# Where the plain weight tiles stand among the short ones in a fused attention block, and when the third head's attention begins

## The chip, the cores and the metric

One Trainium2 chip, one of its cores. The time is device microseconds for one execution of the whole kernel. The kernel before took 740.01 us (median of 3 runs, 738.37 to 742.52).

## The reference

`x` is 256 tokens by 2048 channels, fp32. The block computes, all in fp32 accuracy:

- `h = rmsnorm(x) * g_norm`, then one projection `z = h @ w_in` that yields q, k, v and a gate for 8 differential heads and 8 forgetting heads (head width 128), 8 forget logits and two merge gates of 2048 columns each.
- Forgetting heads: `softmax(q k^T / sqrt(128) + c_q - c_k + causal)` with `c` the running sum of the log forget gates, times v. Differential heads: rotary on 16 of 64 columns, two softmax maps, first minus lambda times second, times v, RMSNorm over the head.
- Each head's output is multiplied by SiLU of its gate; the two branches are projected by `w_proj_a` and `w_proj_b`, merged by two sigmoid gates, projected by `w_out`, added to `x`, and normalized once more.

## The kernel before

**The product.** Every fp32 product is made of three: weight and activation are each split in a high and a low part (`w_hi` + `w_lo`, `hT_hi` + `hT_lo`), and TensorE multiplies high by high, high by low, and low by high.

**The jobs.** The weights come in 326 tiles of 128 x 1024, called jobs, in one fixed order. Five parties work through this same order, each in its own instruction queue: SyncE issues the load of the raw tile (L372 to L392), ScalarE rounds it to `w_hi` (L720), VectorE subtracts to get `w_lo` (L956), TensorE multiplies by `w_hi` (L420, L421) and then by `w_lo` (L435 or L488). There are 4 places for raw tiles and 4 for split tiles. So ScalarE's split of job n + 4 waits until TensorE has finished job n, and the load into a raw place waits until VectorE has done with the job four loads earlier.

**Plain and short jobs.** In a plain job (`tile`, L423) a tile meets both halves of the tokens: 12 matmuls of 512 columns. From job 28 to job 247 the order is made of 11 chunks of 20 jobs. A chunk holds the 8 plain jobs of one head's projection, which accumulate in PSUM banks Z0 and Z1, and 12 short jobs (`sum_tile`, L454) of 6 matmuls each. The short jobs compute the merge gates and two of the heads by a scheme of seven block products (forms P1, P5, P6, P3, P7, P4, P2, four short jobs each) in place of eight. In forms P5, P6, P7 and P4 the weight tile is itself a sum or a difference of blocks, and VectorE makes it first (`add`, L963: lines L969 and L971), five jobs ahead. After some forms VectorE folds a bank into the result (L973). `HEAD_STEPS` (L49) says at which of the 20 steps the plain jobs stand; `SUM_STEPS` are the others.

**Queue order.** In the iteration of job n VectorE does, in this order: the fold if a form ended with n, the add of job n + 5 if it is one, the split of job n + 4, and its pieces of attention. ScalarE does: the evacuation of Z0 and Z1 if n is the last plain job of a chunk (L722 to L726, it waits for TensorE's end of n), the split of job n + 4, its pieces of attention.

**Evacuation.** The first plain job of the next chunk writes Z0 and Z1 again, so TensorE waits there (`banks_free`, L439) for the evacuation.

**Attention.** Each head b has a job X (`X_AT`) and a job Y (`Y_AT`), five jobs later. After job X TensorE transposes the gated output of head b - 2 (L544), the probabilities of head b - 1 (L526) and q and k of head b (L501). After Y it multiplies the values of head b - 1 (L535) and makes the scores of head b (L514, L517). At Y VectorE gates the output and takes the row maxima of the scores (L1101, L1103); one job later ScalarE takes the exponentials (L810, L812). When the maxima of a forgetting head are there, GpSimd makes the bias of the next one (L1368, L1373). For heads 3 to 15 the jobs X and Y are given by `X_ALONE`; those of heads 0 to 2 are written out.

Of the kernel before, what the change touches and what calls it, by code (L numbers as in the profile page):

```python
# [35 lines left out]
N_HEADS = 2 * HEADS  # L36
# [6 lines left out]
FOX2_JOB = FOX_JOB + 16  # L43
DIFF_JOB = FOX2_JOB + 8
# [1 line left out]
LAST_JOB = OUT_JOB + 30  # L46
JOBS = LAST_JOB + TILES

HEAD_STEPS = (0, 3, 5, 8, 10, 13, 15, 17)  # L49
SUM_STEPS = [u for u in range(MIXED) if u not in HEAD_STEPS]  # L50
FOX_STEPS, FOX_SUM_STEPS = (0, 2, 4, 5, 8, 11, 14, 15), (1, 3, 6, 7, 9, 10, 12, 13)
OUT_PLAIN = [(2, j) for j in range(TILES)] + [(0, j) for j in range(4, TILES)] + [(1, j) for j in range(4, TILES)]
# [7 lines left out]
SUM_OF = {job: s for s, job in enumerate(SUM_JOB)}  # L60
X_ALONE = {**{3 + c: MIXED_JOB + MIXED * (c + 1) + 4 for c in range(3)},
           **{b: MIXED_JOB + 3 * MIXED + 4 + 16 * (b - 5) for b in range(6, N_HEADS)}}
X_AT = {21: 0, 28: 1, 38: 2, **{job: b for b, job in X_ALONE.items()}, FOX2_JOB + 1: N_HEADS, DIFF_JOB + 1: N_HEADS + 1}
Y_AT = {25: 0, 33: 1, 43: 2, **{job + 5: b for b, job in X_ALONE.items()}, FOX2_JOB + 5: N_HEADS}

C_ZERO, C_MASK, C_TRI, C_IDENT, C_ONE = 0, P, 2 * P, 3 * P, 4 * P
C_COS, C_SIN, C_BF, C_GS, C_LAM = 5 * P, 5 * P + 16, 5 * P + 32, 5 * P + 40, 5 * P + 41
# [8 lines left out]
def head_job(h, j):  # L76
    c = ALONE.index(h)
    if c == 0:
        return j
    return PLAIN_JOB + j if c == 2 else MIXED_JOB + MIXED * (c - 3) + HEAD_STEPS[j]  # L80

# [61 lines left out]
def build(nc, x, xT, xg, consts_in, w_main, w_fl, g_final, out):  # L143
# [11 lines left out]
    with ctx:  # L155
# [262 lines left out]
        def _(pe):  # L418
# [72 lines left out]
            def head_transposes(h):  # L491

                if h < HEADS:
                    wait_z(pe, h)
                else:
                    pe.wait_ge(rope_ready, h - HEADS + 1)
                if h >= 2:
                    pe.wait_ge(og_ready, h - 1)
                for i in range(2):
                    for m in range(M_TILES):  # L500
                        mm = pe.transpose(A[:, (2 * i + m) * P:(2 * i + m + 1) * P],  # L501
                                          z_of(h)[:, m, i * HD:(i + 1) * HD], ident)
                mm.then_inc(qkT_done, 1)
# [52 lines left out]
            def attention(job):  # L556

                if job in X_AT:
                    b = X_AT[job]
                    if b >= 2:  # L560
# [3 lines left out]
                    if b < N_HEADS:  # L564
                        head_transposes(b)
                if job in Y_AT:
                    b = Y_AT[job]
                    if b >= 1:
# [140 lines left out]
        def _(act):  # L709
# [80 lines left out]
            def head_qkT(h):  # L790

                act.wait_ge(qkT_done, h + 1)
                act.activation(qk0T[:], A[:].rearrange("p (i n) -> p i n", i=2)[:, :, 0:P], ACT.Copy)
                act.activation(qkT_hi[:], A[:, P:4 * P], ACT.Copy).then_inc(qkT_hi_ready, 1)
# [5 lines left out]
            def tanh(h):  # L800

                wait_z(act, h)
                act.activation(gate_tanh[:], z_of(h)[:, :, 3 * HD:4 * HD], ACT.Tanh, scale=0.5).then_inc(tanh_ready, 1)

            def exps(h):

                act.wait_ge(max_ready, max_count(h + 1))
                maps, scale = 1 if h < HEADS else 2, -1.0
                for i in range(maps):
                    act.activation(probs[:, i, 0:P], probs[:, i, 0:P], ACT.Exp, bias=neg_max[:, 2 * i:2 * i + 1],  # L810
                                   scale=scale, accum_out=sums[:, 2 * i:2 * i + 1])
                    ins = act.activation(probs[:, i, P:3 * P], probs[:, i, P:3 * P], ACT.Exp,  # L812
                                         bias=neg_max[:, 2 * i + 1:2 * i + 2], scale=scale,
                                         accum_out=sums[:, 2 * i + 1:2 * i + 2])
                ins.then_inc(exp_done, 1)

            def out_square(h):

                act.wait_ge(o_done, h + 1)
                for m in range(M_TILES):  # L820
                    ins = act.activation(og[:, m, :], A[:, m * P:(m + 1) * P], ACT.Square, scale=inv[:, m:m + 1],
                                         accum_out=o_ssq[:, m:m + 1])
                ins.then_inc(o_squared, 1)
# [28 lines left out]
            def attention(job):  # L852

                if job in X_AT:
                    b = X_AT[job]
                    if b >= 2:
# [3 lines left out]
                    if b < N_HEADS:  # L860
                        head_qkT(b)
                if job - 2 in X_AT and 1 <= X_AT[job - 2] <= N_HEADS:
                    tanh(X_AT[job - 2] - 1)
                if job in Y_AT and Y_AT[job] > HEADS:
                    out_square(Y_AT[job] - 1)
                if job - 1 in Y_AT and Y_AT[job - 1] < N_HEADS:
                    exps(Y_AT[job - 1])

# [597 lines left out]
```

## Time and profile before

| quantity | value |
|---|---|
| median of 3 runs | 740.01 us |
| profiled execution, its own time | 740.3 us |
| its span, first to last instruction | 738.5 us |
| TensorE matmuls busy | 723.9 us (98%) |
| VectorE busy | 624.9 us (85%) |
| ScalarE busy | 462.8 us (63%) |
| GpSimd busy | 85.9 us (12%) |
| mean granted TensorE clock | 0.997 |

The span is the profiler's view of the execution; its own time is 1.8 us longer. TensorE's busy share counts matmuls from issue to their modelled end, so that neighbours overlap; a gap that is shorter than that overlap does not show as idle time. The distance from one matmul's start to the next shows it.

### The profile page before, as it was taken

What the parts mean: (1) busy time and instruction counts of PE and PEld (TensorE: products, weight loads), DVE (VectorE), ACT (ScalarE), POOL (GpSimd) and SP (SyncE); (2) the same over time, 40 slices, a digit from 0 to 9 for tenths busy, and PEclk for the clock granted to TensorE, in tenths of its full rate; (3) what the DMA queues carried; (4) which work ended last, traced back from release to release, by engine and by line L of the source; (5) the groups of instructions that cost most, each with busy time, mean ns of one, the idle gap of its engine ahead of it and who ended that gap; (6) DMA issues with size and microseconds to landing.
All of it is one profiled execution on the core that took longest, in us unless ns stands there. A gap on an engine that the chain in (4) does not pass through costs nothing.

```text
span 738.5 us, 9450 instructions
## 1 busy us (share of the span) xinstructions
PE 723.9 (98%) x3454; PEld 599.1 (81%) x3454; DVE 624.9 (85%) x788; ACT 462.8 (63%) x682; POOL 85.9 (12%) x105
## 2 busy tenths in 40 slices
PE   9999999999999999999999999999999999999995
PEld 6998887868888888888888887888877888888884
DVE  6785698897989988989889899899899667799883
ACT  7963666567575766665865667776657544555552
POOL 0000231020202051000102030111030000001030
PEclk9999999999999999999999999999999999999998
DMA  8679356769676795776966867775768655667862
GB/s 334 211 235 322 125 199 229 245 242 349 217 259 229 239 348 208 261 234 235 326 228 216 270 226 260 281 257 202 225 233 266 214 192 191 279 232 246 285 200 114
DMA packets 49822, 178.39 MB, mean 242 GB/s; under 512 B 5544, under 2 KB 5552, under 8 KB 49264
## 3 DMA queue, kind: packets, MB, share of 16 engines
q1 hardware_dynamic: 48656, 174.41, 67.9%
q10 hardware_dynamic: 864, 1.84, 0.7%
q0 software_dynamic: 256, 1.54, 0.6%
q8 instruction: 27, 0.44, 0.2%
q14 instruction: 19, 0.16, 0.1%
HBM read 175.67 MB, written 2.11 MB: 241 GB/s over the span
## 4 chain that ended last, share of the span: by engine, by line
PE 46%; issue 28%; DVE 14%; DMA 6%; POOL 3%; ACT 2%; POOLq 0%; SPq 0%; DVEq 0%; ACTq 0%
PE Z L420 13%; PE Z L421 12%; PE Z L435 10%; DVE w_lo L956 7%; DMA w_raw<-in_w_main 4%; PE Z L488 3%; DVE x_and_g L971 3%; PE Z L594 3%; POOL rope_t L1385 1%; DMA gates<-c_rows_dram 1%; ACT w_hi L720 1%; DVE w_raw L969 1%; DMA c_rows_dram<-c_neg 1%; DVE sum_lo L1090 1%; POOL o_rstd L1397 1%
## 5 line engine op out<-in xcount | busy, mean ns | idle before, releaser
L956 DVE TENSOR_TENSOR w_lo<-w_raw,w_hi 128x1024 fp32r<-128x1024 f32 (+1 forms) x238 | 291.3, 1232 | 64.5 <-ACT w_hi L720 63.2
L720 ACT ACTIVATE w_hi<-w_raw 128x1024 fp32r<-128x1024 f32 (+1 forms) x237 | 245.4, 1044 | 134.9 <-PE Z L435 74.9
L420 PE MATMUL Z<-w_hi,hT_hi 128*128 128x512 f32 (+2 forms) x640 | 242.5, 382 | 2.6 <-ACT z_sb L725 2.3
L421 PE MATMUL Z<-w_hi,hT_lo 128*128 128x512 f32 (+2 forms) x640 | 240.3, 379 | 0.0
L720 ACT ACTIVATE w_hi<-x_and_g 128x1024 fp32r<-128x1024 f32 x88 | 93.2, 1062 | 95.5 <-DVE x_and_g L971 66.6
L420 PEld LDWEIGHTS Z<-w_hi,hT_hi 128*128 128x128 f32 x640 | 120.3, 188 | 26.8 <-ACT z_sb L725 3.1
L421 PEld LDWEIGHTS Z<-w_hi,hT_lo 128*128 128x128 f32 x640 | 120.4, 188 | 21.7
L435 PE MATMUL Z<-w_lo,hT_hi 128*128 128x512 f32 (+2 forms) x512 | 129.7, 376 | 0.0
L956 DVE TENSOR_TENSOR w_lo<-x_and_g,w_hi 128x1024 fp32r<-128x1024 f32 x88 | 108.4, 1233 | 13.0 <-ACT w_hi L720 11.5
L420 PE MATMUL Z<-w_hi,sum_hi 128*128 128x512 f32 x292 | 115.4, 395 | 1.4 <-DVE x_and_g L1193 1.3
L421 PE MATMUL Z<-w_hi,sum_lo 128*128 128x512 f32 x292 | 113.8, 390 | 0.0
L435 PEld LDWEIGHTS Z<-w_lo,hT_hi 128*128 128x128 f32 x512 | 92.3, 188 | 18.2 <-DVE w_lo L956 0.8
L971 DVE TENSOR_TENSOR x_and_g<-w_raw,x_and_g 128x1024 f32<-128x1024 f32 x66 | 82.0, 1242 | 5.7 <-DMA w_raw<-in_w_main 5.6
L420 PEld LDWEIGHTS Z<-w_hi,sum_hi 128*128 128x128 f32 x292 | 54.8, 188 | 14.1 <-DVE x_and_g L1193 1.7
L421 PEld LDWEIGHTS Z<-w_hi,sum_lo 128*128 128x128 f32 x292 | 54.9, 188 | 10.8
L488 PE MATMUL Z<-w_lo,sum_hi 128*128 128x512 f32 x164 | 50.8, 391 | 0.3
L488 PE MATMUL Z<-w_lo,hT_hi 128*128 128x512 f32 x128 | 39.9, 393 | 0.6 <-DVE w_lo L956 0.5
L1397 POOL TENSOR_TENSOR o_rstd<-o_ms,neg_half 128x2 f32<-128x2 f32 x8 | 7.4, 929 | 270.3 <-DVE o_ms L1180 270.3
L488 PEld LDWEIGHTS Z<-w_lo,sum_hi 128*128 128x128 f32 x164 | 30.6, 188 | 7.5 <-DVE w_lo L956 1.1
L435 PE MATMUL Z<-w_lo,sum_hi 128*128 128x512 f32 x128 | 34.4, 390 | 0.8 <-DVE w_lo L956 0.8
L1368 POOL TENSOR_TENSOR bias<-gates,c_nat 128x128 f32<-128x128 f32 (+1 forms) x16 | 14.4, 918 | 169.3 <-DVE neg_max L1103 161.4
L969 DVE TENSOR_TENSOR w_raw<-x_and_g,w_raw 128x1024 f32<-128x1024 f32 x22 | 27.2, 1238 | 5.3 <-DMA w_raw<-in_w_main 5.2
(219 smaller groups left out, 698.5 us busy)
## 6 DMA issues: line engine op xcount, KB each, us to landing
w_raw<-in_w_main SPq DMA_DIRECT2D x295, 512.0 KB, 4.3
x_and_g<-in_w_main SPq DMA_DIRECT2D x22, 512.0 KB, 7.0
w_raw<-in_w_fl SPq DMA_DIRECT2D x8, 264.0 KB, 3.1
o_T<-in_x SPq DMA_DIRECT2D x1, 2048.0 KB, 8.0
x_and_g<-in_xT SPq DMA_DIRECT2D x4, 256.0 KB, 5.7
gates<-c_rows_dram POOLq DMA_DIRECT2D x1, 1024.0 KB, 8.4
z_sb<-in_g_final SPq DMA_DIRECT2D x1, 1024.0 KB, 10.0
x_and_g<-in_xT ACTq DMA_DIRECT2D x3, 256.0 KB, 7.3
```

The costliest lines, as they stand in the source:

```text
L420: pe.matmul(acc, a_hi, b_hi, start=first, stop=False)
L421: pe.matmul(acc, a_lo, b_hi, start=False, stop=False)
L435: mm = pe.matmul(Z[2 * pair + m][:, 0:n], stat_hi[:, k0 + kk, tok], lo[:, kk], start=False, stop=last and kk == ks - 1 and closed)
L488: mm = pe.matmul(acc[:], stationary(2 * q + kk)[0], lo[:, kk], start=False, stop=2 * q + kk == ks - 1 and (not into_tile or f != P3))
L594: mm = pe.matmul(Z[m][:], x_part[:, 2 * j + kk, m * P:(m + 1) * P], w_part[:, kk], start=(j == 0 and part == 0 and kk == 0), stop=(j == TI ...
L720: act.activation(w_hi[:, t % RING, 0:cols_of(t)], weights(t), ACT.Copy).then_inc(hi_ready, 1)
L956: dve.tensor_tensor(w_lo[:, t % RING, 0:n], weights(t), w_hi[:, t % RING, 0:n].bitcast(fp32), ALU.subtract).then_inc(lo_ready, 1)
L969: dve.tensor_tensor(raw, chain[:, q, :], raw, ALU.subtract).then_inc(added, 1)
L971: dve.tensor_tensor(chain[:, q, :], raw, chain[:, q, :], ALU.subtract).then_inc(added, 1)
L1090: dve.tensor_tensor(sum_lo[:, form], sums_raw[:, form], sum_hi[:, form].bitcast(fp32), ALU.subtract).then_inc(sums_lo_ready, 1)
L1368: pool.tensor_tensor(bias[:, sl].unsqueeze(1), rows.rearrange("p (h n) -> p h n", h=HEADS)[:, h:h + 1, 0:n], c_nat[:, m, h:h + 1].unsqueez ...
L1397: pool.tensor_tensor(o_rstd[:], o_ms[:], neg_half[:], ALU.pow).then_inc(o_rstd_ready, 1)
```

## The change

The plain jobs of a chunk stand at steps 0, 2, 5, 7, 10, 12, 14, 16 in place of 0, 3, 5, 8, 10, 13, 15, 17. Five plain jobs move one step forward, each past one short job. Steps 17, 18 and 19 are then short jobs; before, 18 and 19 were. X of head 2 is job 36 in place of 38, its Y is job 41 in place of 43. All other X and Y keep their job numbers, though some of these jobs are now short where they were plain, or the other way round.

```diff
-HEAD_STEPS = (0, 3, 5, 8, 10, 13, 15, 17)
+HEAD_STEPS = (0, 2, 5, 7, 10, 12, 14, 16)
...
-X_AT = {21: 0, 28: 1, 38: 2, **{job: b for b, job in X_ALONE.items()}, FOX2_JOB + 1: N_HEADS, DIFF_JOB + 1: N_HEADS + 1}
-Y_AT = {25: 0, 33: 1, 43: 2, **{job + 5: b for b, job in X_ALONE.items()}, FOX2_JOB + 5: N_HEADS}
+X_AT = {21: 0, 28: 1, 36: 2, **{job: b for b, job in X_ALONE.items()}, FOX2_JOB + 1: N_HEADS, DIFF_JOB + 1: N_HEADS + 1}
+Y_AT = {25: 0, 33: 1, 41: 2, **{job + 5: b for b, job in X_ALONE.items()}, FOX2_JOB + 5: N_HEADS}
```

## Rows read from the trace of the kernel before

**Rows 1.** The page's first part: busy time, share, instructions of each engine.

```profile
PE 723.9 (98%) x3454; PEld 599.1 (81%) x3454; DVE 624.9 (85%) x788; ACT 462.8 (63%) x682; POOL 85.9 (12%) x105
```

**Rows 2.** Stretches: length, busy time of each engine, granted clock, DMA share, GB/s.

```profile
77.10:121.52 44.42, 42.84 (x207) 35.55 (x206) 40.13 (x52) 30.08 (x49) 11.15 (x13) 1.00 0.51 179
121.52:164.31 42.79, 42.10 (x188) 33.12 (x189) 39.06 (x44) 26.49 (x35) 5.28 (x6) 1.00 0.70 233
164.31:204.79 40.48, 40.48 (x188) 33.80 (x189) 34.75 (x39) 26.85 (x35) 3.70 (x4) 1.00 0.75 273
410.13:452.97 42.84, 41.99 (x203) 34.56 (x202) 39.97 (x52) 27.41 (x45) 6.24 (x7) 1.00 0.73 246
495.55:537.60 42.05, 41.71 (x194) 33.39 (x193) 37.94 (x59) 28.36 (x49) 6.79 (x8) 1.00 0.65 217
```

**Rows 3.** Who waited for whom: total us, times, longest us.

```profile
PE Z L420 <- ACT z_sb L725: 2.3, 2, 1.5
PEld Z L488 <- DVE w_lo L956: 3.3, 6, 0.7
PEld Z L435 <- DVE w_lo L956: 2.0, 4, 1.2
```

**Rows 4.** Groups by shape: busy us, mean ns of one, idle before.

```profile
L956 DVE TENSOR_TENSOR w_lo<-w_raw,w_hi 128x1024 fp32r<-128x1024 f32 x230 | 285.7, 1251 | 60.9 <-ACT w_hi L720 59.7
L725 ACT ACTIVATE z_sb<-Z,rstd 128x512 f32<-128x512 f32 x25 | 15.8, 683 | 8.2 <-PE Z L435 7.2 <-POOL rstd L1353 0.9
```

**Rows 5.** Timeline, TensorE, the starts of jobs 46, 47 and 48: start, length.

```profile
117.17 0.39 PE L420 MATMUL Z<-w_hi,sum_hi 128*128 128x512 f32 x1
118.53 0.39 PE L420 MATMUL Z<-w_hi,sum_hi 128*128 128x512 f32 x1
121.52 0.47 PE L420 MATMUL Z<-w_hi,hT_hi 128*128 128x512 f32 x1 [1.47 <-ACT z_sb L725]
```

**Rows 6.** Timeline, ScalarE and VectorE, ahead of job 48.

```profile
119.28 0.40 ACT L810 ACTIVATE probs<-probs,neg_max 128x128 f32<-128x128 f32 x1 [1.41 <-DVE neg_max L1103]
120.18 1.24 ACT L725 ACTIVATE z_sb<-Z,rstd 128x512 f32<-128x512 f32 x2
122.40 1.23 DVE L956 TENSOR_TENSOR w_lo<-w_raw,w_hi 128x1024 fp32r<-128x1024 f32 x1 [2.01 <-ACT w_hi L720]
```

**Rows 7.** Timeline, TensorE after job 33 and before job 39.

```profile
91.76 0.39 PE L420 MATMUL Z<-w_hi,hT_hi 128*128 128x512 f32 x1
101.30 0.38 PE L544 MATMUL C<-consts,og 128*128 128x128 f32 x2
```

**Rows 8.** Timeline, ScalarE, the last exponential of head 1.

```profile
96.80 0.49 ACT L812 ACTIVATE probs<-probs,neg_max 128x256 f32<-128x256 f32 x1
97.20 0.19 ACT L812 ACTIVATION_READ_ACCUMULATOR probs<-probs,neg_max 128x1 f32 x1
```

**Rows 9.** Timeline, GpSimd's bias of the next head, and VectorE beside it.

```profile
96.28 1.22 DVE L971 TENSOR_TENSOR x_and_g<-w_raw,x_and_g 128x1024 f32<-128x1024 f32 x1
98.77 1.63 DVE L971 TENSOR_TENSOR x_and_g<-w_raw,x_and_g 128x1024 f32<-128x1024 f32 x1
101.80 1.41 DVE L956 TENSOR_TENSOR w_lo<-x_and_g,w_hi 128x1024 fp32r<-128x1024 f32 x1
96.45 2.87 POOL L1368 TENSOR_TENSOR bias<-gates,c_nat 128x128 f32<-128x128 f32 x2 [14.96 <-DVE neg_max L1103]
119.33 1.89 POOL L1368 TENSOR_TENSOR bias<-gates,c_nat 128x128 f32<-128x128 f32 x2 [17.21 <-DVE neg_max L1103]
```

**Rows 10.** Timeline, VectorE and TensorE in the chunk of jobs 48 to 67.

```profile
127.32 3.50 DVE L956 TENSOR_TENSOR w_lo<-w_raw,w_hi 128x1024 fp32r<-128x1024 f32 x3
131.89 1.23 DVE L969 TENSOR_TENSOR w_raw<-x_and_g,w_raw 128x1024 f32<-128x1024 f32 x1 [1.07 <-DMA w_raw<-in_w_main]
147.70 1.23 DVE L971 TENSOR_TENSOR x_and_g<-w_raw,x_and_g 128x1024 f32<-128x1024 f32 x1 [1.39 <-DMA w_raw<-in_w_main]
162.15 0.73 PE L488 MATMUL Z<-w_lo,hT_hi 128*128 128x512 f32 x2 [0.17 <-DVE w_lo L956]
```

**Rows 11.** The loads of L392 from 125 to 165 us, issue to landing.

```profile
DMA to landing us min/median/max: 3.1/4.2/6.7
```

**Rows 12.** Timeline, jobs 207 and 208: TensorE, and ScalarE's work ahead of the evacuation.

```profile
450.60 0.39 PE L420 MATMUL Z<-w_hi,hT_hi 128*128 128x512 f32 x1
452.97 0.47 PE L420 MATMUL Z<-w_hi,hT_hi 128*128 128x512 f32 x1 [0.85 <-ACT z_sb L725]
449.28 1.05 ACT L720 ACTIVATE w_hi<-w_raw 128x1024 fp32r<-128x1024 f32 x1
451.59 1.28 ACT L725 ACTIVATE z_sb<-Z,rstd 128x512 f32<-128x512 f32 x2
```

## The prediction, made before the changed kernel was run

> **What bounds the kernel now.** I read the busy times first: TensorE 98%, VectorE 85% [rows 1]. TensorE's matmuls are the same before and after, so the change can only move TensorE's waits. The stretches come next, cut at the starts of the chunks' first jobs. The third chunk (jobs 68 to 87) takes 40.48 us without a gap; the second has the same jobs and one head's attention too, but takes 42.79, so 2.31 us of it are waits; VectorE is busy 39.06 of the 42.79 us there [rows 2]. The table of waits names two kinds: TensorE for the evacuation of its banks, twice, and its weight loads for VectorE's `w_lo`, ten times [rows 3]. The timelines put a place to them. A short job takes 118.53 - 117.17 = 1.36 us; job 47 starts at 118.53, so job 48 could start at 119.89 and starts at 121.52: 1.63 lost to the evacuation [rows 5]. Job 207 starts at 450.60 and job 208 at 452.97 in place of 451.96: 1.01 lost in the same way [rows 12]. The pool that the change can reach is 1.63 + 2.31 + 1.01 = 4.95 us. The last chunk (jobs 228 to 247, 42.05 us, [rows 2]) has waits for `w_lo` too; I come to it below.
>
> **What moves.** A swapped plain job takes 2.72 us (12 matmuls, twice the short one), so between the two swapped steps TensorE is 1.36 us further on in time for the same job number, and the add of the short job is made one iteration later. At every other step the sums of TensorE time, adds and splits up to that job are what they were. So no job's `w_lo` is wanted earlier than before, and no more VectorE work stands ahead of it. The number of instructions, of loads and of bytes stays. What can change is (A) the evacuation at job 48, (B) VectorE's lateness in the second chunk, (C) the evacuation at job 208.
>
> **A, the first chunk.** ScalarE's exponentials of head 2 wait for VectorE's maxima until 119.28, and only behind them, at 120.18, comes the evacuation of 1.24 us (two of 0.68, [rows 4]) [rows 6]. With Y at job 41 the exponentials stand in iteration 42, and the evacuation in iteration 44, not 45. In its queue it then stands behind the split of job 47 (which waits for an add) and ahead of the split of job 48. Counting VectorE's queue on from 96.28 at 1.14 us for an add and 1.14 to 1.27 for a split (the pitch of such rows, 1.25 long alone, [rows 4]), the add of job 47 ends near 117, ScalarE's split near 118.2, the evacuation near 119.5 and the split of job 48 near 120.5. TensorE would want job 48 at 119.9. Three things take back from the 1.63:
> First, X of head 2. TensorE starts job 34 at 91.76 [rows 7]; with a short, a plain and a short job it now reaches X at 91.76 + 5.44 = 97.20, where before it came at 101.30 [rows 7]. It wants the exponentials of head 1 there, which end at 97.20 + 0.19 = 97.39 [rows 8]. That costs 0 to 0.3 us; I take 0.15, the nearest by these rows. VectorE's queue up to there has the same work as before.
> Second, GpSimd's bias for head 3 begins near 115.7 in place of 119.33, and VectorE is no longer idle beside it. In the row of 98.77, with GpSimd at work, an add takes 1.63 in place of the 1.22 of the row of 96.28 [rows 9]; from 96.28 to 101.72 four operations take about 1.0 us more than their pitch. The cost is 0 (the cover of before) to 1.0; I take 0.5 on TensorE's path, because jobs 46 to 48 have `w_lo` only about 1 us ahead.
> Third, nothing more for the three short jobs: TensorE needs 4.08 us for them, and ScalarE's evacuation and split take 1.24 + 1.05.
> A is 1.63 - 0.65 = 1.0 gained, between 0 and 1.63.
> At the second point a rule of the Trainium skill speaks against the change: "SBUF — State Buffer", section "SBUF: two separate sides", says that an operation of VectorE with two SBUF inputs and one of GpSimd that reads SBUF lock each other out for a whole instruction. By that, four GpSimd operations of about 0.95 us would hold VectorE for up to 3.8 us and A would be a loss of about 2 us (near 741 for the kernel). The rows show VectorE 1.0 us later over such a stretch and GpSimd's pair at 2.87 in place of 1.89, so here the delay is shared and small, and I keep the rows' price.
>
> **B, the second chunk.** VectorE bounds it: at 162.15 TensorE starts on `w_lo` of job 66 having waited for it [rows 10]. VectorE itself has three holes: 2.01 at 122.40 behind the evacuation [rows 6], 1.07 at 131.89 and 1.39 at 147.70, both for a load [rows 10]. The first goes in part with A: VectorE is some 0.9 ahead at job 49. The hole at 131.89 stays: before it was the load of job 55, issued when job 51 was split (127.32 + 1.22 = 128.54). Now the first add is for job 56, whose load is issued one split later, at 129.68 - 0.9 = 128.8; with the median 4.2 us to landing [rows 11] it starts at 133.0, but one split of before has already been done by then, so that after both adds and splits VectorE is only 0.15 ahead. The hole at 147.70 was job 62's load. Now job 61's load is issued near 139.5, lands near 143.7 and is wanted near 144.3: it closes, 1.39 gained. So `w_lo` of jobs 66 and 67 comes 0.15 + 1.39 = about 1.6 earlier, and since VectorE sets the time there, job 68 starts 1.6 earlier, of which A is 1.0 and B adds 0.6. A load takes 3.1 to 6.7 us [rows 11]: the slowest at job 61 gives 6.7 - 4.2 = 2.5 back (B is -1.9), and with no hole at all the whole 2.31 goes. I take the median.
>
> **C, job 208.** X of head 12 is job 204, before short and now the last plain job. Before, ScalarE did the split of job 208 (449.28), the four copies of attention, and then, at 451.59, the evacuation [rows 12]. Now the evacuation stands ahead of the split of 208: from about 449.4 to 450.65, and TensorE can start job 208 at 451.96. The split then ends at 451.7, and the copies (some 1.4 us) and the split of job 209 at about 454.6, just when TensorE comes there. That puts 0.1 to 0.2 on job 209. C is 1.01 - 0.15 = 0.85, between 0 and 1.0.
>
> **The rest.** In the last chunk the adds, folds and attention up to VectorE's iteration 241 are the same sum, so its waits stay: 0. The other chunk ends start without a wait.
>
> **Sum.** 1.0 + 0.6 + 0.85 = 2.45. The profiled execution's own time is 740.3, so 737.85; the median of the runs shown is 0.3 lower: 737.5.
>
> **The rivals.**
> *Data-bound second chunk.* VectorE waits for loads in place of ScalarE: what A gives is lost by job 68, and only C stays: 740.0 - 0.85 = 739.2. For it: two of the three holes are loads [rows 10], and the loads are issued by VectorE's own progress. Against it: the order of the adds after job 56 leaves each load longer.
> *All waits go.* Loads land early, GpSimd costs nothing: 740.0 - 4.95 = 735.1. For it: only 2.01 + 1.07 + 1.39 = 4.5 us of holes [rows 6, 10] keep VectorE late at job 66, and the change needs just half of them. Against it: VectorE's work in the two chunks is 40.13 and 39.06 us [rows 2], so margins stay thin.
> *Slower: the lead runs dry after three short jobs.* At step 16 ScalarE evacuates (1.24) ahead of the split of the next chunk's first plain job, and TensorE covers one plain job less (1.36): 2.6 us per chunk end where VectorE is late, and four ends are (jobs 48, 68, 208, 248). 4 x 2.6 = 10.4 lost, the evacuation waits of 2.64 gone: 747.8. It decides from 0.6 per end (2.45 / 4). Against it: my count at job 48 has the split ready at 120.5 where TensorE comes at 120.5, at 208 ready 0.3 before, so an end costs 0.2 at the most.
> *It doesn't do what it says:* something else holds ScalarE at the chunk's end, and both evacuation waits stay: 740.0.
>
> **How the numbers follow.** Forecast 0.38, data-bound 0.28, all waits go 0.22, slower 0.08, no effect 0.04. 0.5% is 3.7 us, about what a measurement can tell. Faster by more means below 736.3: all waits go, and the forecast's own lower tail (0.06), 0.28. Slower by more: above 743.7, 0.06. The rest is 0.66. The range takes in 735.1 and 739.2; upward it goes to the slow load on top of the forecast (737.5 + 2.5 = 740.0) with the 1.2 that the runs shown differ by beside it. It runs from 734.9 to 741.2.
>
> **What would show it.** Right: no wait for `z_sb` ahead of jobs 48 and 208; jobs 77.10 to 48 in about 43.4 us; the second chunk at about 42.2; X of head 2 near 97.3; the last chunk near 42.05 again. Wrong: a new wait for `w_hi` at a chunk's first job (the slower rival), or a longer hole before an add in the second chunk (the data-bound one), or X of head 2 more than 0.5 us late.

## The result, and the profile after

The changed kernel is slower: 741.27 us (median of 20 executions, 739.39 to 744.82) against 739.40 for the kernel before (20 executions, 736.97 to 743.02), a ratio of 1.0029 with a 95% interval of 1.0016 to 1.0041. Forecast was 0.3% faster; measured is 0.3% slower, 0.07 us above the range. The profiled execution of the changed kernel has an own time of 743.39 us (before 740.3), so it lies 2 us above its own median, and what it shows has to be held against the times. Two executions of e9 below (1477.67 and 1477.81 us) and one of e11 (1218.53) took far longer than all others, and the medians and ratios given there are without them. The page's first part, which answers to [rows 1]:

```profile
PE 725.2 (98%) x3454; PEld 600.0 (81%) x3454; DVE 625.4 (84%) x788; ACT 461.8 (62%) x682; POOL 82.2 (11%) x105
```

The same work. The stretches by chunk, the changed kernel, in the order of [rows 2] (first, second, third, ninth chunk, last):

```profile
77.09:119.52 42.43, 42.43 (x207) 35.69 (x206) 39.98 (x53) 30.75 (x49) 12.99 (x12) 1.00 0.52 186
119.52:163.40 43.88, 41.71 (x190) 33.25 (x188) 39.66 (x44) 25.90 (x35) 5.59 (x4) 1.00 0.72 240
163.40:203.88 40.48, 40.48 (x189) 33.80 (x189) 34.58 (x38) 27.39 (x36) 3.63 (x4) 1.00 0.73 260
410.20:453.43 43.23, 42.51 (x204) 34.48 (x202) 39.01 (x52) 26.17 (x41) 5.26 (x7) 1.00 0.71 243
495.99:538.31 42.32, 41.81 (x194) 33.47 (x193) 39.19 (x58) 28.35 (x49) 8.22 (x12) 1.00 0.65 229
```

Against [rows 2]: the first chunk is 1.99 shorter, the second 1.09 longer, the third equal, the ninth 0.39 longer, the last 0.27 longer. Between them one job (158) came 0.94 late, as single jobs do with either order (with the old one job 159 lost 1.29 in the profile of e2 below). That makes 0.71 in sum, by which job 248 starts later. The rest of the 3.09 us between the two profiled executions comes behind the last chunk. The waits of the changed kernel, from its table (total us, times, longest):

```profile
DVE x_and_g L971 <- DMA w_raw<-in_w_main: 9.6, 7, 2.5
DVE w_raw L969 <- DMA w_raw<-in_w_main: 5.9, 5, 2.2
PEld Z L488 <- DVE w_lo L956: 4.9, 6, 1.8
PEld Z L435 <- DVE w_lo L956: 3.7, 5, 1.2
PE Z L420 <- DVE x_and_g L1193: 2.4, 1, 2.4
```

TensorE's wait for `z_sb` [rows 3] is gone from the table: both evacuations are early enough. On the other side its weight loads wait longer for `w_lo` (8.6 us in place of 5.3), and VectorE's adds wait for loads from memory. A wait of 2.4 us stands ahead of job 256, where the kernel before has 1.3 (below).

**The first chunk** did what the change says. Timelines of the changed kernel: TensorE at X of head 2 and at job 48, ScalarE, GpSimd and VectorE ahead of job 48 (start, length, and in brackets the idle time before it):

```profile
96.85 0.38 PE L544 MATMUL C<-consts,og 128*128 128x128 f32 x2
119.52 0.39 PE L420 MATMUL Z<-w_hi,hT_hi 128*128 128x512 f32 x1
114.69 0.40 ACT L810 ACTIVATE probs<-probs,neg_max 128x128 f32<-128x128 f32 x1 [1.08 <-DVE neg_max L1103]
116.86 1.25 ACT L725 ACTIVATE z_sb<-Z,rstd 128x512 f32<-128x512 f32 x2
114.74 2.87 POOL L1368 TENSOR_TENSOR bias<-gates,c_nat 128x128 f32<-128x128 f32 x2 [13.39 <-DVE neg_max L1103]
115.72 2.97 DVE L956 TENSOR_TENSOR w_lo<-x_and_g,w_hi 128x1024 fp32r<-128x1024 f32 x2
```

The evacuation starts at 116.86, 3.3 us earlier than in [rows 6], and job 48 starts at once, 2.00 us earlier than in [rows 5]. X of head 2 has no wait.

**The second chunk** took half of that back. VectorE, then TensorE near the chunk's end:

```profile
132.25 1.23 DVE L969 TENSOR_TENSOR w_raw<-x_and_g,w_raw 128x1024 f32<-128x1024 f32 x1 [2.16 <-DMA w_raw<-in_w_main]
143.85 1.23 DVE L969 TENSOR_TENSOR w_raw<-x_and_g,w_raw 128x1024 f32<-128x1024 f32 x1 [0.89 <-DMA w_raw<-in_w_main]
158.92 0.73 PE L488 MATMUL Z<-w_lo,hT_hi 128*128 128x512 f32 x2 [1.36 <-DVE w_lo L956]
161.19 0.73 PE L488 MATMUL Z<-w_lo,hT_hi 128*128 128x512 f32 x2 [0.61 <-DVE w_lo L956]
```

The first hole is twice that of [rows 10] (2.16 in place of 1.07), the second is still there (0.89 in place of 1.39), and TensorE waits 1.36 and 0.61 where it waited 0.17.

**Job 208.** TensorE at the `w_lo` of job 206 and the starts of jobs 207 and 208, then ScalarE's evacuation and its split of job 208:

```profile
451.22 0.73 PE L488 MATMUL Z<-w_lo,hT_hi 128*128 128x512 f32 x2 [0.62 <-DVE w_lo L956]
451.78 0.40 PE L420 MATMUL Z<-w_hi,hT_hi 128*128 128x512 f32 x1
453.43 0.47 PE L420 MATMUL Z<-w_hi,hT_hi 128*128 128x512 f32 x1
451.08 1.25 ACT L725 ACTIVATE z_sb<-Z,rstd 128x512 f32<-128x512 f32 x2
452.23 1.06 ACT L720 ACTIVATE w_hi<-w_raw 128x1024 fp32r<-128x1024 f32 x1
```

The wait for the evacuation [rows 12] is gone. But jobs 205 and 206 now wait for `w_lo`, 0.36 + 0.90, and job 208 starts 0.29 late: ScalarE's split of it stands behind the evacuation and ends at 453.29, and TensorE starts at 453.43. In sum 1.55 us in place of 1.01.

**Behind the last chunk.** Ahead of job 256 TensorE waits until VectorE has read a PSUM bank out (the gate of the forgetting branch, L1193). TensorE's first matmul of job 256, and the last longer hole of VectorE before it, in the changed kernel and then in the kernel before:

```profile
559.41 0.76 PE L420 MATMUL Z<-w_hi,sum_hi 128*128 128x512 f32 x1 [2.40 <-DVE x_and_g L1193]
550.21 1.23 DVE L971 TENSOR_TENSOR x_and_g<-w_raw,x_and_g 128x1024 f32<-128x1024 f32 x1 [2.13 <-DMA w_raw<-in_w_main]
```

```profile
557.81 0.47 PE L420 MATMUL Z<-w_hi,sum_hi 128*128 128x512 f32 x1 [1.31 <-DVE x_and_g L1193]
548.62 1.23 DVE L971 TENSOR_TENSOR x_and_g<-w_raw,x_and_g 128x1024 f32<-128x1024 f32 x1 [0.96 <-DMA w_raw<-in_w_main]
```

The load came 1.2 us later to its add, VectorE to the gate, and TensorE to job 256.

The stretches around it, first the changed kernel, then the kernel before; the third number from the end is the granted clock of TensorE as a share of 2.4 GHz:

```profile
556.90:559.40 2.50, 0.10 (x1) 0.02 (x1) 2.50 (x6) 2.50 (x5) 0.00 (x0) 0.96 0.78 249
559.40:562.70 3.30, 3.29 (x8) 2.62 (x9) 3.30 (x4) 0.94 (x1) 0.00 (x0) 0.51 0.66 254
562.70:565.00 2.30, 2.30 (x12) 1.88 (x11) 0.95 (x2) 1.08 (x2) 0.00 (x0) 1.00 0.85 280
```

```profile
557.80:561.00 3.20, 3.19 (x14) 2.67 (x15) 3.20 (x4) 1.12 (x3) 0.00 (x0) 1.00 0.59 193
```

After the longer wait TensorE ran 3.3 us at 0.51, the 1.2 GHz level: 8 matmuls where the kernel before does 14. So the wait costs 1.1 more by itself, and the clock 1.48 on top (job 257 starts 1.60, then 3.08 later than before). These two, 2.6 us, are most of what separates the two profiled executions; the next section shows how often that happens.

### The profile page after: what moved, and what is told of

It is laid out like the page before. It is cut to its first block, busy times and chain, and to the rows that moved or that the text cites. A ratio compares the mean times of both kernels' runs of the same rounds, so it can differ in the third digit from the quotient of the medians.

```text
span 741.6 us, 9450 instructions
## 1 busy us (share of the span) xinstructions
PE 725.2 (98%) x3454; PEld 600.0 (81%) x3454; DVE 625.4 (84%) x788; ACT 461.8 (62%) x682; POOL 82.2 (11%) x105
## 4 chain that ended last, share of the span: by engine, by line
PE 57%; DVE 24%; DMA 10%; ACT 5%; issue 3%; POOL 0%; SPq 0%; DVEq 0%; POOLq 0%; ACTq 0%
PE Z L420 16%; PE Z L421 16%; DVE w_lo L956 12%; PE Z L435 12%; DMA w_raw<-in_w_main 8%; DVE x_and_g L971 5%; PE Z L488 4%; ACT w_hi L720 3%; PE Z L594 3%; DVE w_raw L969 2%; DMA gates<-c_rows_dram 1%; PE A L535 1%; DVE sum_lo L1090 1%; ACT z_sb L725 1%; DMA c_rows_dram<-c_neg 1%
## 5 line engine op out<-in xcount | busy, mean ns | idle before, releaser
L1368 POOL TENSOR_TENSOR bias<-gates,c_nat 128x128 f32<-128x128 f32 (+1 forms) x16 | 16.3, 1036 | 167.2 <-DVE neg_max L1103 159.5
```

The lines of the kernel that those rows point to most:

```text
L1368: pool.tensor_tensor(bias[:, sl].unsqueeze(1), rows.rearrange("p (h n) -> p h n", h=HEADS)[:, h:h + 1, 0:n], c_nat[:, m, h:h + 1].unsqueez ...
```

## The experiments

The second number with each is the ratio to the kernel before, in the same series of runs, with its 95% interval. The kernel before had medians of 739.32 to 739.79 there. Where two kernels are set against each other, I take the difference of their distances from the kernel before; such a difference is good to a little over 1 us. "New order" means the new `HEAD_STEPS`, "old order" the former ones. Several kernels give each chunk its own order:

```diff
-HEAD_STEPS = (0, 3, 5, 8, 10, 13, 15, 17)
+NEW_CHUNKS = (0,)          # differs from kernel to kernel
+STEPS = [(0, 2, 5, 7, 10, 12, 14, 16) if c in NEW_CHUNKS else (0, 3, 5, 8, 10, 13, 15, 17) for c in range(len(ALONE) - 3)]
```

### Which part of the edit, which chunks

**Steps alone: e1_steps_only.** New order in all chunks, attention of head 2 where it was.

```diff
-X_AT = {21: 0, 28: 1, 36: 2, ...
-Y_AT = {25: 0, 33: 1, 41: 2, ...
+X_AT = {21: 0, 28: 1, 38: 2, ...
+Y_AT = {25: 0, 33: 1, 43: 2, ...
```

> The new places of the plain jobs in all eleven chunks, but X and Y of head 2 at jobs 38 and 43 as before. Theory 1 (the order of adds and splits makes VectorE wait longer for loads, in the second, seventh and ninth chunk, and the wait for the fox gate at job 256 gets so long that TensorE's clock falls): about as slow as the change, +1.5 to +3 us against before, the holes before adds again near 15 us in sum, job 68 later than 163.4. Theory 2 (the earlier attention of head 2 does the harm): near before, within 1 us, or faster. The evacuation wait at job 48 shrinks by one short job in both, from 1.63 to about 0.3.

Measured: 740.67 us, 1.0022 (1.0009 to 1.0036). In its profile job 48 starts 2.19 earlier than before, without a wait: the moved steps alone free the evacuation. The second chunk takes 44.34.

**Attention alone: e2_xy_only.** The kernel before with X and Y of head 2 at jobs 36 and 41.

> Only X and Y of head 2 moved to jobs 36 and 41, the plain jobs as before. Theory 1: the evacuation wait at job 48 goes (-1.6), and nothing else changes much: -0.5 to -2 us against before, no clock drop at job 256. Theory 2: slower than before by 1 us or more.

Measured: 738.10 us, 0.9980 (0.9969 to 0.9992). Job 48 starts 1.03 earlier, with 0.12 of a wait left of 1.63, and the second chunk (old order) takes 42.27. So each half of the change removes the evacuation's wait by itself, the attention's half with no loss elsewhere, the steps' half with one.

**New order in the first chunk alone: e3_first_chunk** (`NEW_CHUNKS = (0,)`, attention moved).

> New places of the plain jobs in the first chunk (jobs 28 to 47) alone, with X and Y of head 2 at 36 and 41; the ten other chunks as before. Theory 1: keeps the 2.0 us gained by job 48 and gives back at most the part that the second chunk's loads take: -1 to -2.5 us against before. Theory 2: like before or slower.

Measured: 738.13 us, 0.9985 (0.9972 to 0.9997), 1.66 us faster, the same as e2, so the new order in the first chunk brings nothing on top of the earlier attention that these times can tell. Job 48 starts 1.98 earlier. The whole loss, 1.87 + 1.66 = 3.5 us, thus comes from the new order in the second to the eleventh chunk.

**All but the last chunk: e4_not_last_chunk** (`NEW_CHUNKS = (0, 1, ..., 9)`).

> The changed kernel with the last chunk (jobs 228 to 247) as before. If the last chunk's new order makes the wait ahead of job 256 long (its last adds stand one place later, so VectorE comes late to the fox gate): the wait is back at about 1.5 us, the clock does not fall, and the time is about 2.5 us under the changed kernel, near before. If the wait is decided inside jobs 248 to 256 by when the load for job 254 lands: it stays long in some executions whatever the last chunk is, and the time is that of the changed kernel, +1.5 to +2.5 us.

Measured: 740.60 us, 1.0013 (1.0004 to 1.0021): 0.8 above the kernel before, the changed kernel 1.9 above it. The last chunk bears a part, not the whole.

**All but the second chunk: e5_second_old**, and **the first two alone: e6_two_first** (`NEW_CHUNKS = (0, 1)`).

> The changed kernel with the second chunk (jobs 48 to 67) in its order of before. Theory 1a (the second chunk's new order is the main cost: in three profiles of the new order jobs 48 to 67 take 43.9 to 44.5 us, in the two profiles of the old order with job 48 early 42.2): 1.5 to 2 us under the changed kernel, near before (739 to 739.7), the second chunk near 42.2. Theory 1b (each of the chunks with adds at its end costs a little, the second no more than others): under 0.8 us from the changed kernel.

> New places in the first and the second chunk alone, head 2 early. Theory 1a: the second chunk's cost on top of the kernel with the new order in the first chunk alone (738.1): 739.6 to 740.3. Theory 1b: within 0.6 of 738.1, and the rest of the changed kernel's loss lies in the nine later chunks.

Measured: e5 739.20 us, 0.9990 (0.9972 to 1.0008); e6 739.55 us, 1.0000 (0.9986 to 1.0015). The second chunk's new order costs 2.1 us by the one pair (changed kernel against e5) and 1.8 by the other (e6 against e3). The stretches of the second chunk with the old order (e3, e5) and with the new one (e6):

```profile
119.54:161.72 42.18, 41.79 (x189) 33.17 (x189) 40.01 (x44) 26.29 (x35) 4.74 (x5) 1.00 0.72 241
```

```profile
119.28:160.84 41.56, 41.17 (x190) 33.36 (x188) 39.91 (x44) 26.21 (x35) 4.63 (x4) 1.00 0.76 242
```

```profile
119.34:164.05 44.71, 42.03 (x189) 33.09 (x188) 39.57 (x44) 25.88 (x35) 5.59 (x4) 1.00 0.70 235
```

Job 48 starts within 0.3 us in all three; the chunk takes 42.18 and 41.56 against 44.71 (and 43.88, 44.34, 44.47 and 43.56 in the other profiles with the new order; 41.83 to 42.75 in the five others with the old order and job 48 early). VectorE's work is the same, even a little less. Its first hole, in e3 and in e6:

```profile
130.25 1.22 DVE L969 TENSOR_TENSOR w_raw<-x_and_g,w_raw 128x1024 f32<-128x1024 f32 x1 [1.24 <-DMA w_raw<-in_w_main]
```

```profile
132.58 1.23 DVE L969 TENSOR_TENSOR w_raw<-x_and_g,w_raw 128x1024 f32<-128x1024 f32 x1 [2.82 <-DMA w_raw<-in_w_main]
```

In e3 this is the add of job 55, in e6 that of job 56, one load later. What the view of that one load says of its way from issue to landing, in e3 and in e6:

```profile
DMA to landing us min/median/max: 3.5/3.5/3.5
```

```profile
DMA to landing us min/median/max: 5.1/5.1/5.1
```

These loads are issued close behind one another: in e6 that of job 55 at 126.36 and that of job 56 at 127.50, and they land at 129.69 and 132.56. The add of job 56 comes one split later in VectorE's queue, and its load is issued one split later, so that alone would leave the hole as it was; but the second load of such a group takes longer. In all eight profiles with the old order the add waits for the first load of the group, which took 3.1 to 3.5 us; in the five with the new order it waits for the second, which took 4.3 to 5.1. The hole is 2.07 to 2.82 in all five profiles with the new order here (the split-first kernel below left out), and 0.87 to 1.24 in the eight with the old.

### Are loads the cause?

**Half loads: e7_after_half and e8_before_half.** The loads of jobs 28 to 271 bring only one half of each raw tile (those that go to another buffer, 22 at the most, stay whole), in the changed kernel and in the kernel before; the products then use what the buffer's other half held, so the outputs are not the reference's.

```diff
+                if MIXED_JOB <= job < DIFF_JOB:
+                    sp.dma_start(raw_slot(job)[:, 0:CHUNK], source(job)[:, 0:CHUNK]).then_inc(raw_loaded[r % RAW], 16)
+                    return
```

> The changed kernel with the loads of jobs 28 to 271 into the raw ring cut to the first half of their columns; the other half of the raw tile is what the load before left there, so those weights are not the reference's. Everything else is the same work. If waits for loads (in the changed kernel 12 holes of VectorE, 15.5 us in sum) carry the loss, it vanishes: as fast as the kernel before with the same cut, within 0.7 us, and some 3 to 5 us under the whole-load one. If it is the order of VectorE's and ScalarE's own queues, the loss against before with the same cut stays at 1.5 to 2.5 us.

> The kernel before with the same cut of the loads (half of the columns of those tiles stay what they were). Its holes ahead of adds (10, 10.8 us in sum) go; the evacuation waits at jobs 48 and 208 stay, since they come from ScalarE waiting for VectorE's maxima. 1 to 3 us under the kernel before. If it stays at 739.4, waits for loads cost TensorE nothing in it.

Measured: e7 732.97 us (732.59 to 734.11), 0.9909 (0.9888 to 0.9930); e8 731.92 us (731.63 to 732.62), 0.9895 (0.9873 to 0.9917). Their second chunks:

```profile
119.77:160.79 41.02, 40.83 (x190) 33.49 (x188) 39.47 (x44) 26.02 (x35) 5.60 (x4) 1.00 0.41 129
```

```profile
120.08:160.53 40.45, 40.45 (x188) 33.80 (x189) 39.05 (x44) 26.41 (x35) 5.29 (x6) 1.00 0.42 130
```

With short loads the second chunk of the kernel before has no wait left (40.45, as the third chunk, though VectorE is busy 39.05 of it), and even its evacuation wait at job 48 is mostly gone (1.44 earlier). So what [rows 2] showed as waits for VectorE were late loads, handed on. I had expected e8 to save 1 to 3 us and the evacuation waits to stay; it saved 7.5.

The changed kernel is still 1.05 slower with half loads. It also has less to gain there, since job 48 starts only 0.31 earlier in e7 than in e8. So the new order costs 1.05 + 0.31 = 1.4 us with half loads where it costs 3.5 with full ones: about three fifths of the loss hang on the loads, and two fifths stay with half of them. In e7's profile TensorE comes late at jobs 66, 68, 233 and 248, 0.2 to 0.4 each, and 0.57 of it lies in the second chunk.

The traces show most of what it is there. At Y of head 3 (job 57) GpSimd makes the next bias, four short instructions in two pairs. The second pair and what VectorE does beside its end, in the changed kernel and in e3:

```profile
151.59 2.72 POOL L1373 TENSOR_TENSOR bias<-bias,consts 128x128 f32<-128x128 f32 x2
152.59 1.40 DVE L971 TENSOR_TENSOR x_and_g<-w_raw,x_and_g 128x1024 f32<-128x1024 f32 x1
```

```profile
151.57 1.74 POOL L1373 TENSOR_TENSOR bias<-bias,consts 128x128 f32<-128x128 f32 x2
152.57 0.66 DVE L997 TENSOR_TENSOR gates<-Z,gates 128x512 f32<-128x512 f32 x1
```

In the old order two folds stand there, in the new one an add and a split, and VectorE and GpSimd hold each other up longer. From the gating of the output at Y to the end of the `w_lo` of job 67 VectorE takes 15.0 us in all seven profiles with the new order in this chunk, e7 and e13 (below) among them, and 13.4 in all nine with the old. One add has moved behind Y (1.14, which VectorE has less to do before it); the other 0.46 are this.

### The hole in the second chunk

**Split first: e9_split_first**, and once more as **e13_split_first_again.** The kernel is e6; in one iteration (job 51) VectorE does the split of job 55 ahead of the add of job 56.

```diff
+                if job in (MIXED_JOB + 23,):
+                    split(job + RING)
...
-                split(job + RING)
+                if job not in (MIXED_JOB + 23,):
+                    split(job + RING)
```

> The kernel of e6 (new order in the first two chunks, head 2 early) with one exchange in VectorE's queue: in the iteration of job 51 the split of job 55, whose tile is there, stands ahead of the add of job 56, which waits 2.2 to 2.8 us for its load in all four profiles of the new order. Theory 2a (the second chunk loses because a ready split stands behind an add that waits for a load): the hole shrinks by the split's 1.1 to 1.2 us, job 68 starts about 1 us earlier than in e6's profile (163.0 to 163.3), and the time is 0.6 to 1.2 us under e6's 739.55. Theory 2b (the holes only move: the loads behind it come as late): the next add waits for what was saved, and the time is within 0.4 us of e6's.

Measured: 738.68 us, 0.9995 (0.9978 to 1.0013). The profile read here is that of the same kernel's second series.

> The kernel of e9 again, for a profile of an execution with TensorE at full clock. Theory 2a: the hole ahead of the add of job 56 is 1.1 to 1.7 us, and job 68 starts about 1 us before e6's 164.05. Theory 2b: the second hole, ahead of the add of job 61, takes it: job 68 within 0.4 us of e6's.

Measured: 739.28 us, 1.0000 (0.9988 to 1.0013). VectorE, and the second chunk's stretch:

```profile
130.76 1.23 DVE L956 TENSOR_TENSOR w_lo<-w_raw,w_hi 128x1024 fp32r<-128x1024 f32 x1 [0.79 <-ACT w_hi L720]
131.90 2.36 DVE L969 TENSOR_TENSOR w_raw<-x_and_g,w_raw 128x1024 f32<-128x1024 f32 x2
```

```profile
119.42:162.57 43.15, 41.18 (x190) 33.40 (x188) 39.95 (x44) 25.90 (x35) 5.60 (x4) 1.00 0.72 244
```

No load hole is left there: the add of job 56 starts as soon as the split is done, and the chunk is 1.56 shorter than e6's. So the hole held back a ready split: VectorE's queue is in order, and the add at its head waited for the later load. The Trainium skill says the same of the queue ("TensorE: Matmul & The Clock Gate", section "Architectural detail: the array is 16× 32×32, not 1× 128×128": the queues of ScalarE and VectorE are strictly first in, first out). But not all of the 1.56 is the exchange: the load of job 56 also took only 4.0 us here, 127.59 to 131.58, where e6's took 5.1. In the old order a ready split, that of job 54, stands behind the waiting add too, so what sets the two orders apart is the load that is waited for. In the times, though, e9 is 0.8 under e6 and e13 0.2, less than can be told apart, and 43.15 is still above 42.18 and 41.56. TensorE's wait at job 65 is also still there, 1.56 late by the distance between job starts, against 1.62 to 1.65 in the five other profiles of the new order. The mechanism is seen, its price in the median is not settled.

### The middle and the last chunks

**New in the first and in chunks 2 to 7: e14_mid_new. New in the first and in the last three: e15_late_new.**

> New order in the first chunk and in the third to the eighth (jobs 28 to 47 and 68 to 187), old in the second and the last three, head 2 early. If the later loss lies in the chunks with little lead at their end (188 to 247), this is as e3: 738.1 within 0.5. If it lies in the middle (job 158 waited 0.94 us for VectorE in the changed kernel's profile alone): 738.8 to 739.5.

> New order in the first chunk and in the last three (jobs 188 to 247), old in the second to the eighth, head 2 early. The last three chunks carry the later loss: 738.8 to 739.6, the waits of jobs 205 to 207, 247 and ahead of 256 longer than in e3. If the middle carries it: as e3, 738.1 within 0.5.

Measured: e14 738.06 us, 0.9987 (0.9975 to 1.0000), the same as e3 within the error (0.35 above it): a cost of the middle chunks can't be told. e15 739.82 us, 1.0009 (0.9993 to 1.0026), 2.1 us above e3. TensorE at job 256 in e15, and the stretch:

```profile
557.25 0.47 PE L420 MATMUL Z<-w_hi,sum_hi 128*128 128x512 f32 x1 [2.20 <-DVE x_and_g L1193]
557.89 0.63 PE L420 MATMUL Z<-w_hi,sum_hi 128*128 128x512 f32 x1
```

```profile
557.25:560.50 3.25, 3.25 (x9) 2.52 (x10) 3.25 (x4) 0.93 (x1) 0.00 (x0) 0.56 0.59 202
```

The clock fell again: the slow matmuls begin 0.64 us into job 256, and job 257 comes 1.6 us later. An execution in which this happens has a mean granted clock of 0.995 or less: 4 of 20 of the changed kernel (743.36 to 744.82, four of its six slowest; the other two, 743.73 and 743.85, have 0.997), 3 of 12 of e15, 1 of 12 each of e1, e3 and e5, none of e2, e4, e6 and e14, and 1 or 2 of each series of the kernel before. At 1.5 us each, one in five adds 0.3 to a mean and next to nothing to a median; so the fall explains a part of the slow tail and the profile of the changed kernel, not the 2.1. The wait ahead of job 256, taken from the distance between the starts of jobs 255 and 256, less the 1.36 of a short job, is 2.58 (changed), 2.36 (e15), 1.01 (e1) and 0.90 (e5) with the new order in the last chunk, and 0.45 to 1.48 in seven with the old: suggestive, and too few to call shown.

The last chunk itself shows more. It takes 42.32 to 43.03 us in the five profiles with the new order and full loads, and 41.54 to 42.25 in the nine with the old, 0.8 less in the mean. Most of it sits at its end, and in ScalarE's queue, in the changed kernel and then in the kernel before:

```profile
534.41 0.71 ACT L849 ACTIVATE gates<-gates,half_rstd 128x512 f32<-128x512 f32 x1
535.03 1.04 ACT L720 ACTIVATE w_hi<-w_raw 128x1024 fp32r<-128x1024 f32 x1
537.12 1.05 ACT L720 ACTIVATE w_hi<-w_raw 128x1024 fp32r<-128x1024 f32 x1
538.31 0.47 PE L420 MATMUL Z<-w_hi,sum_hi 128*128 128x512 f32 x1 [0.19 <-ACT w_hi L720]
```

```profile
534.37 1.99 ACT L720 ACTIVATE w_hi<-w_raw 128x1024 fp32r<-128x1024 f32 x2
```

The splits of jobs 247 and 248 follow the last exponentials, in the kernel before at once (its row is both). In the new order a piece of the merge gates (L849, before the change at 528.66, well ahead) stands between, and the evacuation stands ahead of the split of job 248. From the end of the exponentials (the row that reads their sums) to job 248 it is 3.98 to 3.99 us in all five profiles with the new order, and 3.33 in all nine with the old: 0.66 lost. The ninth chunk shows nothing: 42.33 to 43.23 in the six with the new order, 42.45 to 43.24 in the eight with the old.

**The other end of that wait: e10_after_fox9, e11_xy_fox9, e12_first_fox9.** In the stage behind the last chunk the plain job of step 8 goes to step 9, so that job 256 is a short one: on the changed kernel (e10), on e2 (e11) and on e3 (e12).

```diff
-FOX_STEPS, FOX_SUM_STEPS = (0, 2, 4, 5, 8, 11, 14, 15), (1, 3, 6, 7, 9, 10, 12, 13)
+FOX_STEPS, FOX_SUM_STEPS = (0, 2, 4, 5, 9, 11, 14, 15), (1, 3, 6, 7, 8, 10, 12, 13)
```

> The changed kernel with the plain job of the second projection block (its bank is freed by VectorE's gate of the first) one place later, job 257 for 256, and a short job of form P2 in its place, so that TensorE has 1.36 us more to do before it waits. The clock's fall behind that wait (0.51 granted from 559.4 to 562.7 in the changed kernel's profile, mean clock 0.994 to 0.995 in 4 of its 20 executions, against 1 in 35 of the kernel before) should be gone: no execution under 0.996, the top of the spread (743.4 to 744.8) gone. The wait of 0.5 to 2.6 us shrinks by 1.36: the median 0.7 to 1.3 us under the changed kernel.

> The kernel before with head 2 early (e2, 738.1) and that plain job one place later. Each gain stands alone: e2's 1.3 to 1.7 us and the shorter wait at the projection block, 0.6 to 1.3: 737.0 to 737.6, the fastest so far. If the wait there was hidden by VectorE's lateness anyway (VectorE bounds jobs 246 to 256), it stays at 738.1.

> As e11, with the new order in the first chunk as well (e3, 738.13). As e11 within 0.4 us: 737.0 to 737.8, since e2 and e3 gave the same time.

Measured: e10 739.71 us, 1.0008 (0.9995 to 1.0022), 1.5 faster than the changed kernel. e11 737.29 us, 0.9975 (0.9959 to 0.9991), as e2 within the error. e12 736.49 us (735.07 to 739.09), 0.9963 (0.9950 to 0.9977), 1.2 faster than e3 and the fastest of all: it beats the kernel before by 2.8 us and the changed kernel by 4.7. None of the executions compared has a mean clock of 0.995 or less. The step brings 1.5 with the new order in the last chunk (e10) and 1.2 and 0.3 with the old (e12, e11), so it helps either order; that it gives back a part of what the new order costs is not shown. Between e10 and e12 3.2 us are left, 1.8 to 2.1 of them the second chunk's. The other 1.1 to 1.4 are of the later chunks and do not sit at job 256.

## Why the prediction was wrong, by its own steps

**A, the first chunk: right in kind, half in size.** Predicted 1.0 gained, 2.00 in the profile, 1.7 by time (e2, e3). X of head 2 cost 0, not 0.15: the exponentials of head 1 ended at 96.61, ahead of 96.85. GpSimd's bias does slow VectorE: its two splits at 115.72 take 2.97 in place of 2.50, so 0.5 was the right size, but it never reached TensorE: the second split, that of job 47, ended at 118.69, and TensorE came to it at 119.07. The evacuation came earlier than I had counted too (116.86 in place of about 118.2). Of the 2.00 another 0.37 was there by job 34, before any of this; my count had nothing for it.

The rule that the prediction set aside fits these rows after all. GpSimd's four instructions from 114.74 on are recorded with 1.31, 1.59, 1.33 and 0.47 us. The first three end 0.25 to 0.47 us after the instruction of VectorE that was running when they began has ended (at 115.80, 117.14 and 118.69), and the next one of VectorE is longer by about as much (1.42 and 1.63 in place of 1.22). The fourth finds VectorE idle and takes 0.47, and the split that VectorE begins meanwhile takes 1.44. At this place the Trainium skill ("SBUF — State Buffer", section "SBUF: two separate sides") has whichever of the two comes first shut the other out for its whole instruction; this trace agrees. What was wrong was the length that I put into it: each of GpSimd's instructions cost VectorE 0.2 to 0.4 at the most, and not the 0.95 that I had from half of 1.89 [rows 9].

**B, the second chunk: the step that failed.** Its +0.6 was made of a lead that falls from 1.0 to 0.15 at the hole at 131.89 [rows 10], and of 1.39 gained where the one at 147.70 closes. In the profile the first part came about as said: VectorE starts the add of job 57 1.21 earlier than before (134.53 against 135.74), 0.79 of the 2.00 gone. The second part failed: VectorE, having no lead on the loads, came for job 61's at 142.96 and not at 144.3, and waited 0.89. At Y of head 3 it is 1.42 ahead, 0.21 gained in place of 1.39. Then comes a term that I had put at nothing: behind Y it takes 0.46 longer, with GpSimd at work beside it. I had said that no more work stands ahead of any `w_lo`; the work is the same, but it stands beside other work. Job 68 starts 0.91 earlier in place of 1.6.

By the times B is worse, because the right thing to hold it against is the old order with the same early start: e3 reaches job 68 2.59 earlier than the kernel before, and e6 is 1.8 slower than e3. There the first hole counts too: it is longer by 0.8 at the least, since the add waits for the second load of a group (4.3 to 5.1 us) where the old order waits for the first (3.1 to 3.5). The forecast had this loss of lead; it did not see that the old order would have been spared it. With all that, B took A away whole: e6 has the time of the kernel before (1.0000). I had written this outcome down, as the data-bound rival (what A gives is lost by job 68; 739.2, chance 0.28). It is the case that came nearest, and its sign, a longer hole before an add in the second chunk, is there.

**C, job 208: the wait changed its owner.** The 1.01 of [rows 12] is gone, as said. But the evacuation came at 451.08 and not at 449.4, since the split of job 207 ahead of it waited for VectorE's add, and so the split of 208 was 0.29 late. Jobs 205 and 206 wait 1.26 for `w_lo` besides. My sum looked at the evacuation and ScalarE alone. 0.85 forecast, -0.4 in the profile; over all profiles with full loads this chunk is the same in either order, so C is worth about 0.

**The rest, counted as 0: failed.** For the middle chunks 0 holds (e14). The last three cost about 2 us (e15 against e3). The profiles put 0.8 of that into the last chunk, 0.66 of it at its end, where a piece of ScalarE's work now stands ahead of a split that TensorE needs; the wait ahead of job 256, which I had not looked at since it stands behind the last moved job, may bear another part. I had argued that the adds and folds are the same sum, so the waits stay. The sum is the same; what differs is which load an add waits for, what runs beside it, and what stands ahead of the last splits.

**The slower rival** put the loss into ScalarE and three short jobs in a row at the chunk ends. It would need 0.6 per chunk end. At job 48 TensorE doesn't wait at all. At jobs 68 and 208 it comes 0.28 and 0.29 late, both times for a `w_hi` whose split stands behind the evacuation: the sign that I had named for this rival, at half the size that it needs. (At job 68 the old order has 0.23 too, for the evacuation; I had called that end free of waits.) At the end of the last chunk the new order has waits for `w_hi` of 0.17 and 0.19 at jobs 247 and 248 that the old one hasn't, and loses 0.66. So its mechanism is there: at that one end it has the size that the rival needs, and over the four ends it comes to 0 + 0.28 + 0.29 + 0.66 = 1.2 in place of 10.4. The sign of the result came out on its side mainly by other mechanisms.

Behind it all is one thing that the rows did not say: e7 and e8 put 8.3 and 7.5 us of the two kernels down to late loads, and nearly the whole spread too (736.97 to 743.02 with full loads, 731.63 to 732.62 with half). The waits of one profiled execution are one draw of that, and I took each as fixed and reckoned with the median latency of [rows 11] for all loads. What stays open: where in the last three chunks their 2 us arise beyond the 0.8 (the wait ahead of job 256 is suggested, not shown), why the load of the add ahead of job 256 comes later in some profiles of the new order, and how much of e13's 1.56 is the exchange and how much the draw.

## What to carry to other kernels

When an in-order queue mixes operations that need a load with operations that don't, look at what stands behind each one that can wait, and at which of a group of loads it waits for: a step moved one place costs nothing in work and can still wait for a load that takes 4.3 to 5.1 us in place of 3.1 to 3.5. Look also at what another engine does at that moment, since the same work can take longer there, and at what moves behind it in the other queues: here 0.6 us of ScalarE's in front of one split cost TensorE 0.66. Before counting on a wait that goes, halve the loads: that tells whether the wait is one of compute or only a late load handed on, and how much of the spread is loads. And try the halves of a change apart: here moving the attention alone gives the gain of the first chunk (0.9980), and with the new order in that chunk alone and one plain job of the later stage moved, 0.9963.

## What the runs showed of the hardware

After a wait of 2.4 us (2.2 in e15) TensorE, at full speed before, ran at the 1.2 GHz level for 3.3 us: the matmuls of 512 columns start every 0.43 us in place of 0.23, and the next job comes 1.5 us later. After a wait of 1.31 us, at the same job in the kernel before, it did not. The Trainium skill describes the pattern ("TensorE: Matmul & The Clock Gate", section "HAM oscillation — how this bites in real kernels": a wait for data between two bursts of matmuls puts the clock back, and it is paid anew each time). The two profiles with such a wait agree; the waits in the example of the Trainium skill are longer than these, and whether every wait of 2.2 us does it no run here shows.

GpSimd's pair at L1368 takes 2.87 in place of 1.89 [rows 9] and its pair at L1373 2.72 in place of 1.74 when VectorE adds or splits beside it to the end, and VectorE's adds and splits take 0.2 to 0.4 longer there. Beside folds, which read a PSUM bank, GpSimd's last instruction took 0.46 (e3), as it does with VectorE idle.

Of the two loads of 512 KB (jobs 55 and 56) that are issued 1.1 us apart after a pause of 3.7 us, the first took 3.1 to 3.7 us to land and the second 4.0 to 5.1, in all fourteen profiles with full loads.
